# Whole expert rows in eight places for the context's half of the joint stretch, and a context further ahead of the latents

## The reference

```
for each of 2 layers, for the context (1 tile of 128 tokens) and the latents (2 tiles):
    h    = rmsnorm(x) * (1 + sc1) + sh1                    # adaLN modulation
    zin  = h @ w_in                                        # inputs of three mixers
    o_a  = latent attention, 16 heads;  latents read the context's cache too
    o_s  = bidirectional Mamba-2 SSD (both directions)     # steps AB, MX, YD, YO, CS
    o_c  = conformer convolution, 31 taps over 1024 channels
    x   += gt1 * ((g_a*o_a + g_s*o_s + g_c*o_c) @ w_out)
    h2   = rmsnorm(x) * (1 + sc2) + sh2
    # PEER layer: 8 heads, top 16 of 128 x 128 product keys per head
    e, g = top16 and softmax of the product-key scores     # 128 experts per token
    act  = gelu(sum_d u[e] * h2) * g                       # u, v: 16384 x 1024 per layer
    x   += gt2 * sum_k act_k * v[e_k]
y = rmsnorm(x)
```

## Time and profile before

| | us |
|---|---|
| median of 3 runs | 4348.84 |
| lowest and highest run | 4343.66, 4358.1 |
| the profiled execution | 4343.93 |
| its span, first to last instruction | 4341.9 |
| PE, DVE, ACT, POOL busy | 2741.0, 2154.8, 843.7, 1212.0 |
| mean granted TensorE clock, share of full | 0.809 |

### The profile page before, as it was taken

The page is one execution under the profiler, slowest core; times in us unless marked ns, Lnnn a source line. Parts: engine busy times, 40 slices in busy tenths (PEclk is TensorE's granted clock), DMA queues, the critical chain, the costliest instruction groups (busy, mean ns, idle before and its releaser), DMA issues. The chain is left out here.

```text
span 4341.9 us, 45455 instructions
## 1 busy us (share of the span) xinstructions
PE 2741.0 (63%) x16862; PEld 1662.9 (38%) x16862; DVE 2154.8 (50%) x5494; ACT 843.7 (19%) x2020; POOL 1212.0 (28%) x1122
## 2 busy tenths in 40 slices
PE   7988987356643455556489889873655434545554
PEld 5667875234332211111166678752442322111110
DVE  2555628334224668555535556283333146775554
ACT  1334431112010011111123343310120001111111
POOL 0001100334333344444300111012343234443442
PEclk9989988678777777786789899886787777777777
DMA  4233553888888699999931425537888887999998
GB/s 174 76 137 127 190 194 113 242 258 262 254 292 255 203 420 402 420 419 420 418 125 68 176 93 206 208 113 234 253 280 272 262 255 243 419 403 419 420 420 329
DMA packets 183708, 1136.94 MB, mean 262 GB/s; under 512 B 20272, under 2 KB 21872, under 8 KB 101052
## 3 DMA queue, kind: packets, MB, share of 16 engines
q0 software_dynamic: 147456, 805.37, 50.4%
q1 hardware_dynamic: 36032, 328.65, 21.4%
HBM read 1128.99 MB, written 4.95 MB: 261 GB/s over the span
## 5 line engine op out<-in xcount | busy, mean ns | idle before, releaser
L2112 POOL DMA_INDIRECT arena<-in_experts_dram,arena x1024 | 1105.3, 1079 | 1764.6 <-PE bank L2200 1290.1
L2200 PE MATMUL bank<-arena,Z 128*32 128x512 f32 x3072 | 615.6, 944 | 1316.8 <-DMA arena<-in_experts_dram,arena 663.8
L2239 DVE CUSTOM_DVE_ANT_0 arena<-arena 128x1024 f32<-128x1024 f32 x768 | 918.6, 1224 | 479.9 <-DMA arena<-in_experts_dram,arena 451.2
L885 PE MATMUL bank<-arena 128*128 128x128 f32 (+1 forms) x4864 | 832.9, 332 | 17.1 <-ACT arena L1435 17.1
L885 PEld LDWEIGHTS bank<-arena 128*128 128x128 f32 x4864 | 747.2, 194 | 131.9 <-issue 51.1
L2200 PEld LDWEIGHTS bank<-arena,Z 128*32 128x32 f32 x3072 | 111.9, 145 | 1674.5 <-issue 1048.0
L1741 DVE SCALAR_TENSOR_TENSOR arena<-arena,vec 128x256 f32<-128x256 f32 (+1 forms) x1152 | 408.6, 421 | 1.3 <-DVE arena L1683 0.4
L2148 ACT COPY arena<-bank 128x512 f32<-128x512 f32 x256 | 140.0, 588 | 1031.9 <-DVE dots L2239 860.6
L2181 PE MATMUL bank<-arena,consts 128*32 128x512 f32 x2048 | 325.0, 717 | 8.8 <-PEq L2338 8.8
L877 PE MATMUL bank<-arena 128*128 128x512 f32 (+1 forms) x684 | 272.8, 558 | 3.4 <-DVE arena L2032 3.4
L2246 DVE TENSOR_TENSOR Z<-gel,arena 128x16 f32<-128x16 f32 x192 | 33.5, 175 | 412.8 <-ACT gel L2154 368.0
(11 more groups left out here) (261 smaller groups left out, 2594.4 us busy)
## 6 DMA issues: line engine op xcount, KB each, us to landing
arena<-in_w_big_dram SPq DMA_DIRECT2D x128, 2048.0 KB, 8.5
arena<-h_rows SPq DMA_DIRECT2D x64, 512.0 KB
arena<-in_experts_dram,arena POOLq DMA_INDIRECT x1024, 17.6
arena<-mod_scratch SPq DMA_DIRECT2D x16, 512.0 KB, 9.4
arena<-in_w_uq_dram SPq DMA_DIRECT2D x6, 768.0 KB, 4.5
arena<-in_w_ukv_dram SPq DMA_DIRECT2D x2, 1024.0 KB, 4.8
arena<-in_h0T_dram SPq DMA_DIRECT2D x2, 1024.0 KB, 10.5
out_new_state_dram<-arena SPq DMA_DIRECT2D x8, 256.0 KB, 2.0
```

The lines of the kernel that those rows point to most:

```text
L885: mm = nc.tensor.matmul(K.bank(name)[:, 0:N], w[:, k, m * P:(m + 1) * P], src[:, k, :], start=k == 0, stop=k == KD - 1)
L2112: nc.gpsimd.indirect_dma_start(K.at(rows[n % R], D if X.split else 2 * D), None, half_rows if X.split else io["experts"], bass.IndirectOff ...
L2200: mm = nc.tensor.matmul(K.ps[ACC[c]][32 * q:32 * q + 32, :], K.Z[:, b % 2, q, 28 - 4 * r:60 - 4 * r], rows[:, c * 512:(c + 1) * 512], star ...
L2239: nc.vector.tensor_tensor_reduce(out=rows, in0=rows, in1=spread[:, b % NH, :], scale=1.0, scalar=0.0, op0=ALU.mult, op1=ALU.add, accum_out ...
```

## The change

Five things are changed.

1. The context's expert rows are gathered whole (8 KB from `experts`, one list of indices), by XG alone; XW is gone. They go to 8 places `rows`: five from 17152 on, one at 36524, and two in the given place of the weight ring. A place is free when the batch's XV is done.
2. `g2` and `fl` move to the place of the latents' attention output (29440). So g2's load moves from XG 0 to XV 6, and waits until the latents' step br 0,1,3 is in its bank.
3. LEAD is 0.8 instead of 0.72.
4. While the context's routing pieces are laid out, pieces of the latents' long convolution are held back, and then put one by one before the latents' next steps.
5. The class `Front` loses `halves`, and the 15 semaphores of row places become 12.

```diff
-LEAD, END = 0.72, 1.0
+LEAD, END = 0.8, 1.0
...
         if self.n == 1:
-            self.spread, self.g2, self.fl = 14080, 17152, 18176
-            self.U = [19200 + D * i for i in range(8)]
-            self.V = [self.h2, 36524, 37548]
+            self.spread, self.g2, self.fl = 14080, 29440, 30464
+            self.rows = [17152 + 2 * D * i for i in range(5)] + [36524]
...
-        if X.split:
-            yield ("XG", b + 1), []
...
-        yield ("XW" if X.split else "XG", b + 1), []
+        yield ("XG", b + 1), []
...
-    at_a, at_b, j = 0.0, 0.0, 0
+    at_a, at_b, j, held = 0.0, 0.0, 0, []
     for x in a_rest:
         out.append((A, x))
-        at_a += 2.8 / (1.0 - lead) if x[0][0] == "route" else length(A, x[0]) / lead
+        routing = x[0][0] == "route"
+        at_a += 2.8 / (1.0 - lead) if routing else length(A, x[0]) / lead
         while j < len(b_rest) and at_b < at_a:
-            out.append((B, b_rest[j]))
+            if routing and b_rest[j][0][0] == "conv":
+                held.append(b_rest[j])
+            else:
+                out.append((B, b_rest[j]))
             at_b += length(B, b_rest[j][0]) / (1.0 - lead)
             j += 1
-    return out, [(B, x) for x in b_rest[j:]]
+    rest = []
+    for x in b_rest[j:]:
+        if held:
+            if x[0][0] == "conv":
+                held.append(x)
+                continue
+            rest.append((B, held.pop(0)))
+        rest.append((B, x))
+    return out, rest
...
-                experts.V += [s * CHUNK + D * i for i in range(4)]
+                experts.rows += [s * CHUNK + 2 * D * i for i in range(2)]
...
-    for half in range(halves):
-        dst = ei[:, half * SLOTS:(half + 1) * SLOTS].rearrange("p (m q) -> p q m", q=4)
-        if halves == 1:
-            steps(nc.vector.tensor_copy(dst, src))
-        else:
-            steps(nc.vector.tensor_scalar(dst, src, 2.0, float(half), ALU.mult, ALU.add))
+    steps(nc.vector.tensor_copy(ei.rearrange("p (m q) -> p q m", q=4), b[:, 0:P].rearrange("p (q m) -> p q m", q=4)))
...
-            if n >= R and X.split and not second:
-                pool.wait_ge(S["dot_done"], n - R + 1)
-            if n >= R and (second or not X.split):
+            if n >= R:
                 pool.wait_ge(S["v_done"], (n - R) // BATCH + 1)
-            col = (X.halves * (n // SLOTS) + second) * SLOTS + n % SLOTS
-            nc.gpsimd.indirect_dma_start(K.at(rows[n % R], D if X.split else 2 * D), None, half_rows if X.split else io["experts"],
-                                         bass.IndirectOffsetOnAxis(ap=ei[:, col:col + 1], axis=0)) \
+            nc.gpsimd.indirect_dma_start(K.at(X.rows[n % R], 2 * D), None, io["experts"],
+                                         bass.IndirectOffsetOnAxis(ap=ei[:, n:n + 1], axis=0)).then_inc(K.landed[n % R], 16)
...
+        if label == ("XV", 6) and X.n == 1:
+            yield label
+            K.kernel.wait_full(sp, ("S", ("br", 0, 1, 3)))
+            sp.wait_ge(K.context.S["mod_stored"], 16 * len(LATE))
+            sp.dma_start(K.at(X.g2, D), broadcast_row(K, X.l, X.c, 5)).then_inc(S["g2_load"], 16)
```

More of the change, by code:

```diff
@@ L106, with __init__ @@
 class Front:
-    def __init__(self, l, mark, tiles, halves):
-        self.l, self.mark, self.tiles, self.halves = l, mark, tiles, halves
+    def __init__(self, l, mark, tiles):
+        self.l, self.mark, self.tiles = l, mark, tiles
         self.n = n = len(tiles)
@@ L334, in __init__, with run_of @@
             self.rows = [28812 + 2 * D * i for i in range(6)] + [2 * D * i for i in range(6)]
-    def run_of(self, ring, k):
+    def run_of(self, k):
+        ring = len(self.rows)
         first = ring + BATCH * (k - 1) if k else 0
@@ L348, in experts_order @@
     yield ("XG", 0), []
-    if X.split:
-        yield ("XW", 0), []
     def spread(b):
@@ L560, in __init__ @@
         self.one = self.C[:, C_EPS + 1:C_EPS + 2]
-        self.landed = [nc.alloc_semaphore(f"rows_landed{s}") for s in range(15)]
-        self.landed_n = [0] * 15
+        self.landed = [nc.alloc_semaphore(f"rows_landed{s}") for s in range(12)]
+        self.landed_n = [0] * 12
         self.w_landed = [nc.alloc_semaphore(f"weights_landed{s}") for s in range(RINGS)]
@@ L581, in count_loads, with landed_at @@
                 self.w_count[p, chunk] = (s, self.w_loads[s])
[L583 to L594, removed]
-    def count_rows(self, X):
[L597 to L602, removed]
+    def landed_at(self, X, n):
+        R = len(X.rows)
+        return self.landed_n[n % R] + 16 * (n // R + 1)
+    def count_rows(self, X):
+        for n in range(BATCH * X.batches):
+            self.landed_n[n % len(X.rows)] += 16
     def begin(self, phase):
@@ L1665, in gates_dve, with permuted_dve @@
     nc.vector.tensor_tensor(ex, ex, sm.unsqueeze(2).to_broadcast([P, PH, TOPK]), ALU.mult).then_inc(perm_in, 1)
-def permuted_dve(K, dve, steps, name, ei, gpm, halves, done):
+def permuted_dve(K, dve, steps, name, ei, gpm, done):
     nc = K.nc
@@ L2083, in front_dve @@
             yield label
-            permuted_dve(K, dve, steps, label, K.at(F.ei, 2 * SLOTS).bitcast(U32), K.at(F.gpm, SLOTS, 4), F.halves, S["permuted"] if F.context else None)
+            permuted_dve(K, dve, steps, label, K.at(F.ei, SLOTS).bitcast(U32), K.at(F.gpm, SLOTS, 4), S["permuted"] if F.context else None)
 def experts_pool(K, X, pool):
     nc, S, io = K.nc, K.S, K.io
-    ei = K.at(X.ei, X.n * X.halves * SLOTS).bitcast(U32)
-    half_rows = io["experts"].rearrange("r (h n) -> (r h) n", h=2)
+    ei = K.at(X.ei, X.n * SLOTS).bitcast(U32)
+    R = len(X.rows)
     for label in K.order:
-        step = label[0]
-        if step not in ("XG", "XW"):
+        if label[0] != "XG":
             continue
         yield label
-        second = step == "XW"
-        rows = X.V if second else X.U if X.split else X.rows
-        R = len(rows)
-        if label == ("XG", 0) and X.n == 1:
+        if label[1] == 0 and X.n == 1:
             pool.wait_ge(K.context.S["permuted"], 1)
-        if label == ("XW", 0):
-            pool.wait_ge(K.context.S["h2_stored"], 16)
             K.kernel.wait_full(pool, K.kernel.ph.last[K.kernel.ph.given])
-        for n in X.run_of(R, label[1]):
+        for n in X.run_of(label[1]):
             if n == SLOTS:
                 pool.wait_ge(S["permuted"], 1)
-            if n >= R and X.split and not second:
-                pool.wait_ge(S["dot_done"], n - R + 1)
-            if n >= R and (second or not X.split):
+            if n >= R:
                 pool.wait_ge(S["v_done"], (n - R) // BATCH + 1)
-            col = (X.halves * (n // SLOTS) + second) * SLOTS + n % SLOTS
-            nc.gpsimd.indirect_dma_start(K.at(rows[n % R], D if X.split else 2 * D), None, half_rows if X.split else io["experts"],
-                                         bass.IndirectOffsetOnAxis(ap=ei[:, col:col + 1], axis=0)) \
-                .then_inc(K.landed[K.place_of(X, n // BATCH, n % BATCH, second)], 16)
+            nc.gpsimd.indirect_dma_start(K.at(X.rows[n % R], 2 * D), None, io["experts"],
+                                         bass.IndirectOffsetOnAxis(ap=ei[:, n:n + 1], axis=0)).then_inc(K.landed[n % R], 16)
 def experts_sp(K, X, sp):
@@ L2129, in experts_sp @@
             b = label[1]
+            if b == 0:
+                sp.wait_ge(K.context.S["permuted"], 1)
+                sp.wait_ge(K.context.S["h2_stored"], 16)
             if b >= NH:
@@ L2271, in experts_dve @@
             yield label
-            permuted_dve(K, dve, steps, label, K.at(X.ei + X.halves * SLOTS, X.halves * SLOTS).bitcast(U32),
-                         K.at(X.gpm + 4 * SLOTS, SLOTS, 4), X.halves, S["permuted"])
+            permuted_dve(K, dve, steps, label, K.at(X.ei + SLOTS, SLOTS).bitcast(U32), K.at(X.gpm + 4 * SLOTS, SLOTS, 4), S["permuted"])
     dve.wait_ge(S["fold_ready"], 4 * X.n)
```

30 lines of the change are left out of this document (9 added, 21 removed).

## The result

The changed kernel took 4232.31 us (median of 3 runs, 4231.17 to 4249.85) beside 4348.84 before: a ratio of 0.9742, 95% interval 0.9695 to 0.9788. That is 116 us faster, where 364 had been forecast, and outside the forecast range of 3860 to 4130. Its profiled span is 4229.1 us at a mean granted clock of 0.824.

The account below looks back on a forecast made before the run. DMA was taken as the joint stretch's nearer bound (621 us, engines 467); after the change 515 / 0.86 = 599 us, so 21 + (760 - 599) = 182 a layer, 364 in both: 4343.9 - 364 = 3980 us, range 3860 to 4130.

Parts of the forecast that it names:

- the sum: Joint stretch: DMA needs 515 us, at share 0.86 it lasts 599 instead of 760; with the start, 182 us saved a layer.
- Whole rows save 119 us of transfer: Gathers of the joint stretch: 8 KB packets at 317 ns cut the gather queue from 444 to 325 us.
- the forecast's own sign of being wrong: Profile of the changed kernel: the forecast is wrong if the gather queue still needs over 400 us.
- a packet's price does not fall beside weights: Rival on the joint stretch's gathers: they keep their 444 us, a layer saves 77, 4190 us in all; chance 0.08.
- The start: Ahead of and in the context's choice: the new order makes gathers begin 21 us earlier, 14 plus 7.
- The rows no longer late for V: V steps of the joint stretch: whole places give rows two batch periods to land; late rows had cost 293 us.
- The engines' bound of 496 us: Joint stretch without late rows: the engines' own order needs 467 us, plus 29 for work moved in.
- g2: Load moved to XV 6 behind br 0,1,3: that step ends earlier (16% against 23%), so SyncE does not stand there.
- the place ring: Rival on the eight row places: held from issue to V, they become the bound; slower, up to 4606 us; chance 0.04.
- The forecast's own range: Whole kernel, main forecast (chance 0.52): 3910 to 4050 us, for shares 0.90 to 0.81 and start 10 to 30 us earlier.

Follow-up runs that it names:

- e1: The changed kernel with each h2 row stored four times, so a spread's source has 16 outer steps instead of 4: 3920.82 us, ratio 0.9013.
- e6: The kernel before (half rows, old order) with h2 stored four times and spreads of 16 outer steps: 3959.1 us, ratio 0.9109.
- e16: The kernel before with eight copies of each h2 row and spreads of 32 outer steps: 3898.54 us, ratio 0.8962.
- e11: The changed kernel with eight copies of each h2 row and spreads of 32 outer steps: 3850.13 us, ratio 0.8855.
- e4: The kernel before with the new order only (LEAD 0.8, convolution pieces held back), half rows kept: 4286.46 us, ratio 0.9842.
- e3: The changed kernel with the old order (LEAD 0.72, nothing held back), whole rows kept: 4263.1 us, ratio 0.9789.
- e8: The changed kernel with the old order (LEAD 0.72, nothing held back) and spreads of 16 outer steps: 3937.36 us, ratio 0.9054.
- e2: The changed kernel without the spreads of batches from 3 on, leaving out part of the work; those left keep four outer steps: 3871.31 us, ratio 0.8896.
- e13: The changed kernel with 36 copies of each h2 row, every spread packet reading its own row, 16 outer steps of 8: 3968.05 us, ratio 0.9125.
- e10: The changed kernel with 32 copies of each h2 row, every spread packet reading its own row, 128 outer steps: 3890.83 us, ratio 0.8955.
- e14: The changed kernel with all 128 partitions of a spread reading one row, 128 outer steps, leaving out part of the work: 3861.77 us, ratio 0.8879.
- e17: The changed kernel with eight copies of each h2 row, spreads of 32 outer steps and LEAD 0.76: 3825.59 us, ratio 0.8807.

## Why the prediction was wrong

**The step that failed: the sum.** It took what the transfers need as the mean over 16 engines (621 us before, 515 after) and let the stretch be that at a share of 0.86. But a transfer is complete only with its slowest share. A spread's 128 packets of 4 KB take 194 ns each in the packet records, 32 x 128 x 0.194 = 795 us of engine time: 50 us when spread over 16 engines, 199 on four. So, as an estimate, those four carry 577 (the 56.7 and 24.6% of 710) - 50 + 199 = 726 us, as long as the stretch itself (710), and the other twelve 527, or 0.74 of it. (It is rough: the same sum for the kernel before, with 238 ns a packet, gives 804 us for a stretch of 760.) A mean share of 0.82 was full use of four engines, and less for twelve. The sum could have been made from the kernel's own code and the earlier trace rows: 56 MB of "hardware" packets contain 17 MB of spreads with a 4 in the access pattern. e1 shows it: 312 us from the access pattern and its store. Not all of that is balance: the two queues' own time also falls from 577 to 529 us (95.8% of 552), as packets get quicker, which is some 50 of the 158 us by which the stretch is shorter. No run separates the two.

**Whole rows save 119 us of transfer: mis-sized.** It measured 10 us a layer (e6 to e1) to 18 (e16 to e11). In the changed kernel the queue kept 403 us; over 400 was the forecast's own sign of being wrong. The 444 us and the 262 GB/s of the earlier trace rows were not the price of half rows but of spreads beside them: from the kernel before to e6 the same half rows went from 444 to 370 us. The Trainium skill's rule (DMA: Bandwidth & Descriptors, section Specifications: from 512 B on the line rate is reached), which I weighed and set aside, is nearly right here: 4 KB rows cost 348 us where 8 KB rows cost 330. The comparison of the earlier trace rows with the earlier trace rows had changed two things at once, the packet size and the company. The rival "a packet's price does not fall beside weights" (0.08, 4190 us) was the nearest in time, 42 us off, and right in that the queue's time stayed high (403 us after), though not in its reason, since spreads and not weights are the company that costs.

**The start: right.** Forecast 21 us earlier, measured 28, and 20 with the order alone (e4, 732.3).

**The rows no longer late for V: right, and worth less.** The landings (22.6 us median, 24.2 before) now hold up the dots instead: every batch needs its rows for the dots first, and with whole rows the dots' wait is the only one. The engines' bound of 496 us had been read as if it could be met independently of DMA.

**g2, the place ring: right at next to nothing.** SyncE issues g2's load 0.6 us after the weights ahead of it (893.02 and 892.44), so it does not stand there. The load lands 35.9 us later (median of the two layers), and VectorE waits 10 us for it in both layers together. GpSimd's longest waits are for V (517.9 us), without being the bound. The ring is no bound: e1 and e11 use the same eight places and run a layer 158 and 190 us faster.

**Not foreseen: weights.** They land late (31.8 us median, 18.3 before), which costs TensorE 112 us. The two more chunks in the stretch are not the cause. With whole rows and the old order (e3, 18 chunks) they land late as well, and TensorE waits 80 us. With half rows and the new order (e4, 20 chunks) it waits for none. The loads of weights in e3 (761 to 1460 us), in e4 (732 to 1474 us), and e3's longest wait for them (us, times, longest us):

```profile
arena<-in_w_big_dram SPq DMA_DIRECT2D x18, 2048.0 KB, 37.9
...
arena<-in_w_big_dram SPq DMA_DIRECT2D x20, 2048.0 KB, 19.8
...
PE bank L868 <- DMA arena<-in_w_big_dram: 41.1, 5, 22.6
```

So it comes from whole rows beside spreads on four engines; e8, whole rows with even spreads, has next to none. No run shows by which step whole rows delay the weights.

**The size of the forecast was there, but not in the change.** 3980 us was reached by the kernel before with one access pattern changed (3959.1), and the change is worth 38 to 48 us beyond that. Both then keep the DMA engines busy for 0.96 to 0.97 of the stretch.

**A sum that does not come out.** The forecast's own range ended at 4050 us for a share of 0.81 and a start 10 us earlier; by its own terms that is 515 / 0.81 = 636, so 4343.9 - 2 x 134 = 4076 us. The measured time lies beyond either.

**Still open:** e2, with three spreads a layer, is not faster than e11 with all of them (3871 from two runs, and 3850; the intervals overlap a little). Part of it is the three that are left, in four steps: over the 60 us from 727 a gather's packet takes 426 ns in e2 and 317 in e11, and after that 325 and 322. LEAD 0.76 was tried only with even spreads. Why 16 outer steps slow the gathers' packets while 32 do not is shown only as such (e13 beside e10 and e11). The Trainium skill (SBUF — State Buffer, section on Door 1: The DMA port swizzle) says that a transfer's partitions decide which of 16 ports it writes through. If each engine is dealt 8 neighbouring partitions under 16 steps, and 4-partition pieces otherwise, the two would differ in ports; the runs fit that but none measures a port.

## What to carry to other kernels

A DMA share is a mean over 16 engines. Before using it as a bound, look at the slices for valleys at 0.25 or 0.5, and read the outermost dimension of every load's source and destination: here a broadcast from four rows ran on four engines, and each of them carried four times what an even split would have given it. A transfer waits for its slowest engine, and the weights beside it came late too (31.8 us instead of 13.6). When two rows of a trace differ in two things (packet size and what runs beside), don't price the change by one of them; and when several causes of a wait are together, fix the cheapest first, since the value of the others shrinks (here from 116 to 38 us).

## What the runs showed of the hardware

- With loads of 4 outer steps among the others, exactly four packets are under way in 16% of the stretch, at a DMA share of 0.25 (1019 to 1031 us); with 8 steps it is eight packets, in 8%. 8 and 16 steps took 160 and 312 us off the same kernel.
- With all engines in use a load with 16 outer steps still slows gathers beside it (322 to 439 ns a packet), one with 32 or 128 does not (318 and 315); e11 is 71 us faster than e1.
- A packet of a gathered 4 KB row takes 169 ns on average (e16) and that of an 8 KB row 322 ns (e11), or 348 and 330 us for 134 MB: halving a row costs 5% here.
- Reading the same DRAM row for all 128 partitions slows nothing beside it: gathers' packets take 319 ns, with separate rows 315 (e14, e10).
- The granted clock of the stretch is 0.78 in the changed kernel, where TensorE is busy for 390 of 710 us, and 0.87 in e17, where it is busy for 364 of 507. What that is worth was not measured.
